# Adding the causal mask of an attention with TensorE instead of VectorE, in a hybrid decoder step

## The reference

```python
proj = rms_norm(x) @ w_in
# attention heads: 8 query heads of 64 in 2 groups; three branches per head
s = q @ k.T * HEAD_DIM ** -0.5
p = softmax(where(kpos <= qpos, s, -1e30))      # causal: the part that is changed
o = g_cmp * o_cmp + g_sel * o_sel + g_win * o_win
# RWKV-7 heads: a recurrence over 512 tokens, done in chunks of 64
mixed = concat([o, o_rwkv]) @ w_out
x = x + rms_norm(mixed)
x = x + rms_norm(conv_ffn(rms_norm(x)))
```

## Time and profile before

| | us |
|---|---|
| median of 3 runs (lowest, highest) | 2517.59 (2514.95, 2524.11) |
| profiled execution, its own time | 2526.33 |
| its span, first to last instruction | 2524.5 |
| TensorE busy | 2076.7 (82%) |
| VectorE busy | 1237.8 (49%) |
| ScalarE busy | 717.9 (28%) |

### The profile page before, as it was taken

The page is one execution under the profiler, slowest core; times in us unless marked ns, Lnnn a source line. Parts: engine busy times, 40 slices in busy tenths (PEclk is TensorE's granted clock), DMA queues, the critical chain, the costliest instruction groups (busy, mean ns, idle before and its releaser), DMA issues.

```text
span 2524.5 us, 55955 instructions
## 1 busy us (share of the span) xinstructions
PE 2076.7 (82%) x22574; PEld 1885.5 (75%) x22574; DVE 1237.8 (49%) x2079; ACT 717.9 (28%) x1336; POOL 156.2 (6%) x233
## 2 busy tenths in 40 slices
PE   6996697876688799999679967978666787999995
PEld 5995686744467699999669856867445587999995
DVE  4223658562863644452332337486638535444523
ACT  3221223231333322242132112232314333222421
POOL 1000011100110001000000000101001000101000
PEclk9997798968798799999879877989787998999998
DMA  3264223122222122223122632222222221223232
GB/s 123 92 142 136 77 83 95 52 65 71 75 63 92 47 93 93 93 84 101 46 83 92 146 121 86 85 85 69 57 76 71 71 79 51 93 93 93 87 98 71
DMA packets 172778, 216.50 MB, mean 86 GB/s; under 512 B 39009, under 2 KB 138594, under 8 KB 171106
## 3 DMA queue, kind: packets, MB, share of 16 engines
q1 hardware_dynamic: 172514, 212.87, 28.0%
HBM read 204.57 MB, written 16.59 MB: 88 GB/s over the span
## 4 chain that ended last, share of the span: by engine, by line
PE 60%; DVE 19%; SPq 11%; issue 6%; ACT 2%; DMA 1%; DVEq 0%; ACTq 0%
PE ps L812 15%; PE ps L814 15%; PE ps L813 15%; SPq L694 7%; PE ps L1105 4%; SPq L691 3%; PE ps L880 1%; DVE arena L1804 1%; DVE smp L1882 1%; DVE arena L1840 1%; PE ps L853 1%; DVE x L2023 1%; DMA ring<-in_w 1%; DVE arena L1630 1%; PE ps L934 1%
## 5 line engine op out<-in xcount | busy, mean ns | idle before, releaser
L812 PE MATMUL ps<-hm_hi,ring_hi 128*128 128x260 f32 x2432 | 695.6, 286 | 57.6 <-DVE hm_lo L1594 57.6
L814 PE MATMUL ps<-hm_hi,ring_lo 128*128 128x260 f32 x2432 | 693.6, 285 | 0.0
L813 PE MATMUL ps<-hm_lo,ring_hi 128*128 128x260 f32 x2432 | 691.3, 284 | 0.0
L1587 DVE TENSOR_TENSOR ring_lo<-ring,ring_hi 128x1024 fp32r<-128x1024 f32 x200 | 245.0, 1225 | 707.7 <-ACT ring_hi L1257 707.7
L812 PEld LDWEIGHTS ps<-hm_hi,ring_hi 128*128 128x128 f32 x2432 | 465.0, 191 | 61.1 <-issue 61.1
L813 PEld LDWEIGHTS ps<-hm_lo,ring_hi 128*128 128x128 f32 x2432 | 464.5, 191 | 0.0
L814 PEld LDWEIGHTS ps<-hm_hi,ring_lo 128*128 128x128 f32 x2432 | 464.2, 191 | 0.0
L1257 ACT ACTIVATE ring_hi<-ring 128x1024 fp32r<-128x1024 f32 x200 | 211.8, 1059 | 696.9 <-PE ps L814 675.2
L812 PE MATMUL ps<-hf_hi,ring_hi 128*128 128x260 f32 x704 | 202.5, 288 | 8.2 <-DVE hf_lo L1594 8.2
L814 PE MATMUL ps<-hf_hi,ring_lo 128*128 128x260 f32 x704 | 200.7, 285 | 0.0
L813 PE MATMUL ps<-hf_lo,ring_hi 128*128 128x260 f32 x704 | 200.5, 285 | 0.0
(11 more groups left out here) (371 smaller groups left out, 3302.1 us busy)
## 6 DMA issues: line engine op xcount, KB each, us to landing
ring<-in_w SPq DMA_DIRECT2D x202, 512.0 KB, 3.5
arena<-in_kv_cmp SPq DMA_DIRECT2D x96, 128.0 KB, 2.2
extra<-in_kv_cmp SPq DMA_DIRECT2D x80, 128.0 KB, 2.2
slot<-in_kv_cmp SPq DMA_DIRECT2D x80, 128.0 KB, 2.2
out_win_old<-in_win SPq DMA_DIRECT2D x16, 511.0 KB, 9.5
slot<-in_k_sel SPq DMA_DIRECT2D x96, 64.0 KB, 1.9
arena<-in_k_sel SPq DMA_DIRECT2D x96, 64.0 KB, 1.9
extra<-in_v_sel SPq DMA_DIRECT2D x96, 64.0 KB, 1.9
```

The source lines that it names most:

```text
L812: mmul(out, wh, hi[:, k, cols], start=(k == 0), stop=False)
L813: mmul(out, wh, lo[:, k, cols], start=False, stop=False)
L814: last = mmul(out, wl, hi[:, k, cols], start=False, stop=(ci == len(chunks) - 1 and k == k1 - 1))
L1587: v.tensor_tensor(ring_lo[:, n % RING, :], r, ring_hi[:, n % RING_HI, :], SUB).then_inc(S["w_lo"], 1)
```

## The change

The mask is added by TensorE: after the two score products of a unit, two matmuls with the identity as weights and the 128x128 mask constant as moving operand accumulate into the last 128 columns of the same two banks. VectorE's add is gone and its step `mask` is only the row maximum. The planner's costs follow: 0.55 us more for `scores`, 0.5 us less for `mask`.

```diff
@@ att_thread
-            put(u, "scores", "PE", 0.3 + 0.25 * w, (u - 1, "evac") if u > first else (t, "cdone"))
+            put(u, "scores", "PE", 0.85 + 0.25 * w, (u - 1, "evac") if u > first else (t, "cdone"))
             if u > first:
                 put(u - 1, "values", "PE", 0.2 + 0.35 * w, (u - 1, "evac"))
-            put(u, "mask", "DVE", 0.8 + 0.25 * w, (u, "scores"))
+            put(u, "mask", "DVE", 0.3 + 0.25 * w, (u, "scores"))
@@ TensorE, att, step "scores"
                         for g, r in enumerate(rows):
-                            last = mmul(ps[:, 4 + g, 0:(t + 1) * P], nsa[r, i, t * P:(t + 1) * P],
-                                        nsa[r, 6 + 2 * br, 0:(t + 1) * P], start=True, stop=True)
+                            mmul(ps[:, 4 + g, 0:(t + 1) * P], nsa[r, i, t * P:(t + 1) * P],
+                                 nsa[r, 6 + 2 * br, 0:(t + 1) * P], start=True, stop=False, skip_group_check=True)
+                        for g in range(GROUPS):
+                            last = mmul(ps[:, 4 + g, t * P:(t + 1) * P], ident, K("causal"), start=False, stop=True, skip_group_check=True)
                         last.then_inc(S["sc_mm"], 1)
@@ VectorE, att, step "mask"
                         dve.wait_ge(S["sc_mm"], n + 1)
-                        d = ps[:, 4:6, t * P:(t + 1) * P]
-                        o.do(v.tensor_tensor(d, d, K("causal").unsqueeze(1).to_broadcast((P, 2, P)), ADD))
                         o.go(v.tensor_reduce(nm, ps[:, 4:6, 0:w], AX, MAX, negate=True))
```

## The result

The changed kernel takes 2622.09 us (median of 4 runs, 2621.59 to 2622.70) against 2517.95 us for the kernel before, a ratio of 1.041 with a 95% interval of 1.0391 to 1.043. That is 104 us more, outside the predicted range and on the side of rivals 3 and 4. The profiled execution's span is 2620.4 us, 95.9 us more than before.

What follows compares the result with a forecast made beforehand. The paired stage was taken as time to `win_v` (TensorE and VectorE alternating), a fixed SyncE load train and a tail. Added 4.7 less removed 5.0 us a layer, -0.6 us for both, gave 2517 us, range 2471 to 2565.

Steps and rivals of the forecast that it cites:

- rival 3: Paired stage: the list puts more ahead of the sample or behind the last load, 13 us a layer, 2543 us; chance 0.24.
- Rival 4: First stretch: TensorE bounds it and takes all added work with nothing back, list unchanged, +21, 2538 us; chance 0.07.
- What bounds the kernel: Paired stage: time to `win_v`, a fixed-length train of loads, and a tail; only the first and third can move.
- a train of loads: Selected branch's page loads on SyncE: 14 steps took 204.9 us, 14.6 each; should stay at 14.6 in every case.
- a tail: Work behind the last load, last `var` product to `out`: some 11 us, worth 11 us a layer at most by going.
- The price of the operations: Both layers, order of steps fixed: added 4.7 less removed 5.0 us a layer, -0.6 us in all, ends -10 to +21.
- The removed part: VectorE's mask add, 0.47 us a unit: of 19 units in the first stretch about 11 on the path, 5.0 us a layer.
- the added part: TensorE's mask products in the first stretch: 10.5 us a layer, 45% of it on the path, 4.7 us.
- The price of a pair of products: TensorE, two float32 mask matmuls a unit: 0.55 us, taken from `chunks`, with 0.49 as the other end.
- rival 1: Paired stage: the list keeps its shape and products replace the add at the same price, 2517 us; chance 0.33, the forecast.
- the planner doesn't see the bound: Planner's cost of a selected-branch load: 10.1 us where the trace has 14.6, so its plan is 72 us of loads short.
- rival 2: Paired stage: the list lets the sample go first, `win_v` 14 us earlier a layer, 2489 us; chance 0.31.

Runs made afterwards that it cites:

- experiment 1: Two kernels: the changed kernel with the planner's old costs, 2525.51 us, ratio 1.0016; the kernel before with the new costs, 2620.16 us, ratio 1.0395.
- experiment 1's first kernel: The changed kernel's operations with the planner's old costs, so on the list of the kernel before: 2525.51 us, ratio 1.0016.
- experiment 3: Planner's load formula raised, 14.5 us for 16 transfers: on the kernel before 2494.25 us, ratio 0.988; on the changed kernel 2492.10 us, ratio 0.9875.
- experiment 6: No run: planned spans worked out along given lists; at the changed kernel's costs 491.7 us old list, 484.9 new; with the raised load formula 533.7 against 554.7.
- seed 2: The kernel before with only the seed of the planner's random search set to 2 in place of 0: 2517.47 us, ratio 0.9982.

## Why the prediction was wrong

- **What bounds the kernel: right.** The stage is the time to `win_v`, a train of loads and a tail; the three differences of the queue's rows add up to the measured difference of the spans. The dense stages stayed as they were.
- **The price of the operations: near, but with the wrong sign.** On a fixed list I had -0.6 us with ends -10 and +21; experiment 1 measured +4.3, inside the ends and small, but its interval leaves out zero. The removed part was worth 14.2 us where I had 10.0, the added part 12.5 where I had 9.4. VectorE's and TensorE's parts all but cancel, as the sum had it. On that list VectorE is busy 27.5 us less (I had 28) and TensorE 23.5 more (I had 35).
- **The price of a pair of products: somewhat too low.** I took 0.55 us. Of the 19 pairs in the first stretch of experiment 1's first kernel 8 take 0.55 us from their start to that of the next product, 8 take 0.64 to 0.65, and 3, at the lower clock, 1.15 (last section). Added up that is 13.0 us a layer where I had 10.5. I had counted nothing for the clock, and about 1.8 us of the difference are these three. The chain gives the products 10.0 us a layer, and their measured price is 6.2, where I had put 4.7 on the path.
- **The step that failed: rival 1, "the list keeps its shape", as the likeliest.** I called the planner's choice close to a toss and gave 0.31 to the list that goes the right way and 0.24 to the one that goes the wrong way, more together than to the one that stays, and still forecast no move. The list moved, and experiment 1 puts 3.95 of 4.1% on it. "No row can give the new list" is true, but the kernel's own code gives it: with the new costs `merged_order` puts 21 units ahead of `win_v`, which meets rival 3's own condition.
- **The size of rival 3.** Its condition came true: 21 units ahead of the first `win_v`, from 20 on it was to decide. Its price was one unit and its share, 13.1 us a layer, got by dividing the stretch by its units, as though `att` and `rwkv` moved in step. They are merged by a bias each and move apart: two units went ahead and most of a chunk of `rwkv`, and the train starts 60.6 us late. The range's high end, one such share and one more tail, was too low for the same reason.
- **Rival 4 has fallen.** With the products on the old list the loss is 4 us, not 21.
- **That the planner doesn't see the bound: right.** With the load formula near the trace both kernels gain 1.2%, where the changed one had lost 4% (experiment 3), and with that formula the planner's sum turns against the new list, which it had preferred (experiment 6). The prediction left it at "close to a toss". What the search finds still hangs on small things: a single entry or a seed moves the time by 0 to 2.6%.
- **A reading from the first stretch alone misleads.** Trains that started 29 to 35 us early grew by 14 to 25 us, since what stood ahead of it must still be done. I had priced rival 2 at the full 14 us a layer; seed 2 shows 12.2 gained and 10 of it lost again.
- **Two slips of reading** that change no result: the selected branch's first load starts at 504.05 us, and 530.60 is its second; VectorE's free time under the train is 96 us, not 97.

## What to carry to other kernels

Where a planner orders the work, compare two operations on one and the same order first: here the edit itself was worth 0.16% and the new order 3.95%. If one resource bounds a stage (here SyncE's issue of page loads), its cost in the planner should be near the one in the trace, or the plan optimises something else; here that was one formula, and worth more than the edit. When the order comes from code, run that code before the forecast: it shows without a chip whether the order moves. And before a change in such a kernel is judged, a run or two with another seed tells how far the order alone moves the time.

## What the runs showed of the hardware

Two identity products of float32, 128 rows deep and 128 columns wide, take no fixed time. The timeline of the kernel with the products on the old list has three prices. Followed by `chunks`, at the full clock (granted 1.00 from 342 to 344 us):

```profile
342.63 0.71 PE L1076 MATMUL ps<-cst 128*128 128x128 f32 x4
343.18 1.07 PE L1107 MATMUL ps<-arena,smp 128*128 128x128 f32 x8
```

Followed by a smaller product, at the full clock (granted 1.00 of 2.4 GHz from 305 to 309 us):

```profile
306.97 0.71 PE L1076 MATMUL ps<-cst 128*128 128x128 f32 x4
...
307.62 0.43 PE L1091 MATMUL ps<-arena 31*64 31x128 f32 x4
```

At the lower clock (granted 0.50, that is 1.2 GHz, from 405 to 409 us):

```profile
406.60 1.22 PE L1076 MATMUL ps<-cst 128*128 128x128 f32 x4
407.75 0.69 PE L1091 MATMUL ps<-arena 31*64 31x128 f32 x4
```

From the pair's start to the next product's start it is 0.55 us in the first, 0.65 in the second and 1.15 in the third. Read the same way, four matmuls of `chunks` take 1.00 us in the earlier trace rows (305.64 to 306.64), 0.50 for two. The Trainium skill's figure for a stream ("TensorE: Matmul & The Clock Gate", Back-to-back issue gap), 81 ns a matmul with its weight load, would give 0.32 us for four records, an estimate from that page; the trace does not agree for float32. The three places lie within 100 us in one stretch, so the price of an added product depends on where the list puts it.
